# A weight-stationary kind of its own, 96 columns wide, for experts with 65 to 96 tokens

## The reference

```python
def swiglu(h, wg, wu, wd):
    return jnp.einsum('btf,fd->btd', jax.nn.silu(h @ wg) * (h @ wu), wd)

def moe_ffn(h, router_w, router_b, wg, wu, wd):
    logits = jnp.einsum('btd,de->bte', h, router_w).astype(f32) + router_b
    top_v, top_i = lax.top_k(logits, TOP_K)              # TOP_K = 2, N_EXPERTS = 8
    gates = jax.nn.softmax(top_v, axis=-1)
    combine = jnp.einsum('btk,btke->bte', gates, jax.nn.one_hot(top_i, N_EXPERTS, dtype=f32))
    for e in range(N_EXPERTS):
        y = y + combine[..., e:e + 1] * swiglu(h, wg[e], wu[e], wd[e])
```

## Time and profile before

| | |
|---|---|
| Median of 3 runs | 2071.0 us (2069.66 to 2072.14) |
| The profiled execution | 2071.74 us, span 2069.9 us |
| Granted clock of PE, mean | 0.901 |
| PE busy | 1783.1 us (86%) x10676 |
| PEld busy | 1304.0 us (63%) x10677 |
| DVE, ACT, POOL busy | 411.5, 248.7, 167.5 us |
| HBM read | 473.12 MB |
| Chain that ended last | PE 72%, DMA 14%, DVE 4% |

### The profile page before, as it was taken

The page is one execution under the profiler, slowest core; times in us unless marked ns, Lnnn a source line. Parts: engine busy times, 40 slices in busy tenths (PEclk is TensorE's granted clock), DMA queues, the critical chain, the costliest instruction groups (busy, mean ns, idle before and its releaser), DMA issues.

```text
span 2069.9 us, 25905 instructions
## 1 busy us (share of the span) xinstructions
PE 1783.1 (86%) x10676; PEld 1304.0 (63%) x10677; DVE 411.5 (20%) x759; ACT 248.7 (12%) x491; POOL 167.5 (8%) x201
## 2 busy tenths in 40 slices
PE   6998875756899999788769999889999799997784
PEld 3765444644677777564259999349994399953331
DVE  2033426773201111661000001000001000010002
ACT  2122342112100000231000000010001000010101
POOL 4003105380000000220000000000000000000001
PEclk8998596565899999889889999999999899998997
DMA  9752042000925556505975656999779997789996
GB/s 339 264 214 86 1 123 56 1 1 26 324 81 203 204 183 244 214 11 206 388 267 212 213 213 216 353 392 346 284 274 341 390 390 249 288 318 389 393 391 221
DMA packets 235290, 481.57 MB, mean 233 GB/s; under 512 B 16575, under 2 KB 90691, under 8 KB 234803
## 3 DMA queue, kind: packets, MB, share of 16 engines
q1 hardware_dynamic: 229755, 471.91, 63.0%
q0 software_dynamic: 3904, 5.44, 0.8%
q10 hardware_dynamic: 1568, 3.34, 0.4%
HBM read 473.12 MB, written 7.90 MB: 232 GB/s over the span
## 4 chain that ended last, share of the span: by engine, by line
PE 72%; DMA 14%; DVE 4%; POOL 3%; issue 3%; SPq 2%; ACT 2%; POOLq 0%; DVEq 0%; ACTq 0%
PE bank L1004 70%; DMA ring<-in_moe_w_up 12%; POOL ring L2197 2%; DMA ring<-in_ada_w 1%; POOL other L2206 1%; ACT ring L1486 1%; SPq L2319 1%; SPq L2284 0%; DVE wide L1778 0%; DVE wide L1762 0%; PE bank L1137 0%; DVE wide L2100 0%; DMA ring<-in_cache_fox_logf 0%; SPq L836 0%; SPq L2310 0%
## 5 line engine op out<-in xcount | busy, mean ns | idle before, releaser
L1004 PE MATMUL bank<-wide,ring 128*128 128x144 f32 (+4 forms) x4240 | 697.1, 332 | 27.8 <-issue 15.9
L1004 PEld LDWEIGHTS bank<-wide,ring 128*128 128x128 f32 (+2 forms) x4240 | 618.5, 191 | 106.2 <-issue 40.5
L1004 PE MATMUL bank<-ring,wide 128*64 128x384 f32 (+2 forms) x1600 | 297.6, 529 | 85.1 <-DMA ring<-in_moe_w_up 71.1
L1004 PE MATMUL bank<-other,ring 128*128 128x144 f32 (+3 forms) x2016 | 292.3, 320 | 50.6 <-POOL ring L2197 29.3
L1004 PEld LDWEIGHTS bank<-other,ring 128*128 128x128 f32 (+1 forms) x2016 | 267.9, 194 | 75.6 <-POOL ring L2197 31.1
L1004 PEld LDWEIGHTS bank<-ring,wide 128*64 128x64 f32 (+1 forms) x1600 | 121.4, 158 | 249.6 <-issue 235.6
L1004 PE MATMUL bank<-ring,other 128*64 128x512 f32 x560 | 128.0, 596 | 8.4 <-ACT other L729 8.4
L795 DVE TENSOR_TENSOR other<-other,bank 128x288 f32<-128x288 f32 (+3 forms) x48 | 21.4, 446 | 499.8 <-PE bank L1004 499.8
L777 DVE TENSOR_TENSOR other<-other,bank 64x512 f32<-64x512 f32 (+1 forms) x40 | 24.5, 613 | 457.1 <-ACT other L726 457.1
L2263 POOL TENSOR_TENSOR small<-const 128x1 f32<-128x1 f32 x1 | 0.2, 193 | 1134.1 <-DMA expert_rows<-other 1134.1
L1004 PE MATMUL bank<-ring 128*64 128x64 f32 (+6 forms) x468 | 75.9, 392 | 13.5 <-ACT ring L1486 8.8
(11 more groups left out here) (329 smaller groups left out, 965.5 us busy)
## 6 DMA issues: line engine op xcount, KB each, us to landing
ring<-in_moe_w_gate SPq DMA_DIRECT2D x32, 2048.0 KB, 12.6
ring<-in_moe_w_up SPq DMA_DIRECT2D x32, 2048.0 KB, 16.6
ring<-in_moe_w_down SPq DMA_DIRECT2D x32, 2048.0 KB, 16.7
ring<-in_ada_w SPq DMA_DIRECT2D x24, 2048.0 KB, 13.9
ring<-in_moe_w_gate SPq DMA_DIRECT2D x32, 1536.0 KB, 11.7
ring<-in_moe_w_up SPq DMA_DIRECT2D x32, 1536.0 KB, 15.5
ring<-in_moe_w_down SPq DMA_DIRECT2D x32, 1536.0 KB, 16.4
ring<-in_w_in SPq DMA_DIRECT2D x5, 2048.0 KB, 12.7
```

The source lines that it names most:

```text
L1004: return pe.matmul(out, lhsT, rhs, start=start, stop=stop, skip_group_check=True)
```

## The change

A constant `LEAST` = 96 and a kind LOW between FEW and SOME. An expert with 65 to 96 tokens is done by `tensor_more`, `scalar_more` and `vector_more` with 96 columns in place of 144. On PE, ACT and DVE this is one more body of code, behind the one for FEW, and one more comparison ahead of those for SOME and MANY. Since 96 tokens fit one block of 128 rows, the end of such an item has 8 transposes in place of 16, one copy of rows on DVE in place of two, two copies of 256 columns on ACT, and its two stores split by columns. The plan gets one more operation on DVE.

```diff
-CAP, MID, HALF = 192, 144, 64
+CAP, MID, LEAST, HALF = 192, 144, 96, 64
-FEW, SOME, MANY, NONE = range(4)
+FEW, LOW, SOME, MANY, NONE = range(5)
...
-                pe.transpose(B[c // 4][:, at], outT[:, c, 0:P], ident)
-                m = pe.transpose(B[2 + c // 4][0:k - P, at], outT[:, c, P:k], ident)
+                m = pe.transpose(B[c // 4][0:min(k, P), at], outT[:, c, 0:min(k, P)], ident)
+                if k > P:
+                    m = pe.transpose(B[2 + c // 4][0:k - P, at], outT[:, c, P:k], ident)
...
+            else:
+                act.activation(yrow[0:k, 0, 0:256], B[0][0:k, 0:256], ACT.Copy).then_inc(s("eaT_ready"), 2 * ROUNDS)
+                act.activation(yrow[0:k, 0, 256:512], B[0][0:k, 256:512], ACT.Copy).then_inc(s("out_act"), 1)
...
+            else:
+                for i in range(2):
+                    act.dma_start(slab[bass.ds(row, k), 512 * i:512 * (i + 1)], yrow[0:k, 0, 512 * i:512 * (i + 1)])\
+                        .then_inc(s("rows_out"), 16)
...
-            dve.tensor_copy(yrow[:, 0, 512:D], B[1][:, :])
-            dve.tensor_copy(yrow[0:k - P, 1, 512:D], B[3][0:k - P, :]).then_inc(s("out_dve"), 1)
+            m = dve.tensor_copy(yrow[0:min(k, P), 0, 512:D], B[1][0:min(k, P), :])
+            if k > P:
+                m = dve.tensor_copy(yrow[0:k - P, 1, 512:D], B[3][0:k - P, :])
+            m.then_inc(s("out_dve"), 1)
...
                     with engine.Else():
-                        with engine.If(kind == SOME):
-                            more(it, MID)
+                        with engine.If(kind == LOW):
+                            more(it, LEAST)
                         with engine.Else():
-                            more(it, CAP)
+                            with engine.If(kind == SOME):
+                                more(it, MID)
+                            with engine.Else():
+                                more(it, CAP)
...
             do(TS(kind, load, float(HALF), None, ALU.is_gt))
+            do(STT(kind, load, float(LEAST), kind, ALU.is_gt, ALU.add))
             do(STT(kind, load, float(MID), kind, ALU.is_gt, ALU.add))
```

## The result

The changed kernel takes 2105.2 us, median of 4 runs (2101.37 to 2108.52), the kernel before 2071.6 (2069.66 to 2073.13): ratio 1.0156, 95% interval 1.0141 to 1.0170. The profiled execution has a span of 2101.3 us where the one before had 2069.9, 31.4 us more.

The account below looks back on a forecast made before the run. Item 5 was taken as bound by PE, its neighbours by the DMA. Saving 15.5 us on item 5 and paying 47 us for displaced PE code gave +31.5 on 2071.74: 2102 us, range 2057 to 2116.

Parts of the forecast that it names:

- What bounds item 5, and the floor: Expert with 65 tokens: PE-bound; weight loads floor a record at 112 ns, so rounds fall from 41.16 to 37.6 us.
- The end of item 5: After its last matmuls: dropped second DVE copy, eight fewer transposes and shorter copies save 1.4 us, bounds 0.7 and 1.8.
- the up weights: First round of item 5: they land just in time as the first gate group ends; 0.3 us at most.
- Net of the columns: Item 5's shorter rounds (14.1 us) and shorter end (1.4 us) together save 15.5 us.
- Code as the cost: PE's loop: 168 added matmuls stretch its code from seven blocks to ten, with eight held; refetches cost 47 us.
- the wait isn't code: Rival: PE's wait at item 1 is a jump or plan-value exchange, so only -15.5 remains, 2055 us; chance 0.03.
- ten blocks held: Rival: PE holds ten code blocks, so only first visits cost; 2060 us; chance 0.24.
- the least used block is dropped: Other half of the held rival: PE drops the least used block, only first visits cost; 2060 us; chance 0.24 together.
- Which block is pushed out: PE's code store: placed by number modulo eight, blocks 0 and 8, 1 and 9 displace each other; some 30 more packets.
- take to stay held: ACT's and DVE's new bodies, a tenth of PE's in size, stay in their instruction stores; no cost put on them.
- The sum: Whole program: 47 us of PE code waits less 15.5 us saved, net +31.5 us, 2102 us.
- The clock: PE's granted clock in item 5 stays at 1.00 once it is back; at 0.50 a round would be 75 us.

Follow-up runs that it names:

- e5: The changed kernel without a 144-column body: bodies for 64, 96 and 192 columns, item 3 at 192, code no longer than before; 2114.6 us.
- e4: The kernel before with one threshold moved, so that item 3 (137 tokens) takes the 192-column body, no other code; 2133.7 us.
- e6: The changed kernel with the four rounds of ACT and DVE as a loop of the engine in place of four copies; 2090.4 us.
- e1: The kernel before plus a 96-column body that no item takes, in the code of PE, ACT and DVE; 2133.0 us, ratio 1.0302.
- e3: The kernel before plus a 96-column body that no item takes, in ACT's and DVE's code only; 2095.4 us, ratio 1.0119.
- e9: The kernel before plus 30 unused matmuls, half a block, in PE's code between the few-column and 144-column bodies; 2074.8 us, ratio 1.0009.
- e2: The kernel before plus an unused 96-column body in PE's code only, in front of the 144-column one; 2129.6 us, ratio 1.0289.
- e7: The changed kernel with PE's bodies in the order 96, 144, 192, 64 columns, nothing else changed; 2166.7 us, ratio 1.047.
- e8: The kernel before plus an unused 96-column body in PE's code only, behind the other bodies; 2082.6 us, ratio 1.0051.
- e14: The kernel before with 64 of a round's 168 matmuls doubled at 96 columns inside PE's 144-column body, for 65 to 96 tokens; 2074.2 us, ratio 1.0006.
- e13: The changed kernel with its bodies in the order 64, 144, 192, 96 columns on PE, ACT and DVE; 2099.0 us.
- e12: e13 with the rounds of ACT and DVE as a loop of the engine in place of four copies; 2086.2 us, ratio 1.0065.

## Why the prediction was right, and where only its sum was

- **What bounds item 5, and the floor.** Right. 111.7 ns a record against 112 taken, 37.52 us a round against 37.6. By the rule of the Trainium skill (TensorE: Matmul & The Clock Gate, LDWEIGHTS) it would have been 107 ns and 21.3 us saved; the trace says 111.7 and 14.6.
- **The end of item 5.** 1.4 us forecast, 0.7 found in e5, inside the bounds at their lower edge; the up weights came 0.6 us late, where 0.3 at most was said.
- **Net of the columns.** -15.5 forecast, -14.5 measured by item lengths (e5 against e4, and e6).
- **Code as the cost.** Right, and shown without the change itself: e1 to e3. The count of seven blocks against ten fits what came (no packets after 1120 us before, 15 in the changed kernel), and half a block more, in e9, was enough to bring packets back. The rival "the wait isn't code" fell with e2, "ten blocks held" with the packets of the changed kernel after 1120 us: 15, where the rival wanted hardly any. Its other half, that the least used block is dropped and so only first visits cost (2060 us), fell as to the price; the rule itself is open (below).
- **Which block is pushed out.** Wrong. Placing by number modulo 8 was said to bring some 30 more packets after 1120 us; 15 came. Of the waits of 10 us and more announced before items 3 and 5, item 3 had 6.3 + 2.1 and item 5 none, and item 4 had 11.7 where 3 us was taken. PE's code came to +33 us (e6 less the kernel before, 18.3, and the columns' 14.5) where the sum had 47.
- **ACT and DVE "take to stay held".** Wrong. The step took their bodies' size for an argument, a tenth of PE's, without asking how much these engines hold. It cost 14.8 us, and q14 fetched 57 packets in place of 19. The trace before had a hint: q14's packets are half the size of PE's.
- **The sum.** 47 - 15.5 = +31.5 was forecast and 33 + 14.8 - 14.5 = +33.3 found: about 14 us too many for PE, 15 too few for ACT and DVE. So 2102 against 2105.2 is partly luck; the mechanism and the columns' term were right, two terms were each off by 14 us.
- **By place.** Each term of the forecast put into the item whose length it would change, against the table of lengths: item 0 +11.0 (+7.6), item 1 -3.6 + 3 = -0.6 (-0.1), item 2 +11.0 (+8.5), item 3 3.6 + 1.5 + 3 = +8.1 (+15.2), item 4 +11.0 (+3.7), item 5 3.6 - 15.5 + 3 = -8.9 (-8.5), items 6 and 7 nothing (+2.3 and +5.2, both gone in e6 and so ACT's and DVE's). Items 1 and 5 came out by other parts than these: item 5 had no slow clock at its start and 2.0 us before item 6, but 5.9 us of ACT's code (159.9 against 154.0 in e6). Counted over the waits of the kernel before, those at the borders before items 2 and 4 were put at 3 us each and were 5.7 and 9.9; those before items 3 and 5 were put at 11 each and were 5.0 and nothing.
- **The clock.** 1.00 in item 5, as said; the slow clock after a long wait shows at the small items too (0.91 above), where no price had been put on it.

What stays open is the rule by which a block is dropped, and how many are held. Eight blocks, the least recently used one replaced and the next one fetched when a block is first entered, forecast the time of e7 well (2160 us for 2166.7) and its packets (over 40; 48 came). The rule with the oldest block replaced had the packets of e8 and not its time, and modulo 8 had neither. Seven blocks touched were held in the kernel before; with eight touched, e9 and e14 fetched 6 packets each after 1120 us. But e4 touches no more than seven, and fetched 5. Nor can it be the code and the order of the items alone: e3 has PE's code of the kernel before, word for word, and the same kinds of items in the same order, and fetched 3 packets after 1120 us where that fetched none. Each of these counts is from one profiled execution, and whether another execution of the same kernel fetches the same was not looked at; the changed kernel and e6, with one PE code, do agree (24 packets, the same waits), and so do e13 and e12 (21).

The Trainium skill (Advanced Engine Details and Errata, ISA Cache) gives 32 KB, 128 KB on TensorE, in lines of 16 KB. PE's packets of 16 KB (0.72 MB in 44, in the kernel before) agree with the line; that eight of them are held no run here shows. The Trainium skill (Runtime: NRT & Kernel Launch, Instruction fetch mechanics) warns that a taken branch to code outside the window forces a fetch, which the waits of e7 and e2 bear out. The same section of the Trainium skill calls the memory a FIFO with purely sequential prefetch, which, read literally, would have each jump between the bodies fetch anew; the kernel before jumped between three of them and fetched nothing in 950 us. Here the traces decide.

## What to carry to other kernels

A specialised body for a case costs the code of that case, and in a loop over data-dependent kinds it can be paid again at item after item. Count the instruction blocks that the loop touches (here 722 instructions, 2.8 blocks, a body) on each engine before adding one, look at the packets of the instruction queues after the first visits, and price a new one by an unused copy of the body, which is a small experiment (e1 to e3). Where more code can't be avoided, put the bodies taken most often next to the loop's head and the rare ones last (e8 is 47 us under e2; e13, only 6 under the changed kernel), and keep the rounds of the lighter engines in a loop: between the best and the worst order and form tried here (e12 and e7) lie 80 us, with the same matmuls.

A narrower tile pays only down to the weight load: for 128x128 weights in 32 bits that was 111.7 ns a record, so 96 columns gave 9% of a round, not a third.

## What the runs showed of the hardware that I had not expected

- 168 matmuls that never run cost 58 us in 2071 (e2), or 9 us if they lie behind the others (e8).
- ACT's first read of an item came 23.1 us after PE's start (4.2 in the kernel before), while q14 fetched six packets and the DMA engines were full (e3, 1385 to 1425 us), and PE was held up for 7.9. A lighter engine's code can stop the heavy one in the middle of the work.
- A wait of 10.7 us in front of a DMA-bound item cost 14.4: in the lap behind it the DMA share was 0.68 (0.89 before) and PE's granted clock 0.91 (1.00 before) (e12).
- Identical PE code fetched 0, 3 and 5 packets after 1120 us in three kernels (before, e3 and e4; in e4 item 3 is of another kind).
